# A SwiGLU feed-forward with seven half-block products in place of eight, and its down projection moved behind all gates

## The reference

```python
hn = rmsnorm(x, ln_mix_pre)
x = x + rmsnorm(stick_breaking_mixer(hn, w_qkv, w_o), ln_mix_post)
hn = rmsnorm(x, ln_ffn_pre)
g, u = jnp.split(hn @ w_gu, 2, axis=-1)      # 1024 x 1024 @ 1024 x 5632
y = (jax.nn.silu(g) * u) @ w_down            # 1024 x 2816 @ 2816 x 1024
x = x + rmsnorm(y, ln_ffn_post)
```

## Time and profile before

| | us |
|---|---|
| median of 3 runs | 1355.73 |
| lowest, highest | 1354.17, 1356.25 |
| span of the profiled execution | 1353.8 |
| PE busy | 1317.0 (97%) |
| DVE, ACT, POOL busy | 709.7, 541.8, 330.8 |

### The profile page before, as it was taken

The page is one execution under the profiler, slowest core; times in us unless marked ns, Lnnn a source line. Parts: engine busy times, 40 slices in busy tenths (PEclk is TensorE's granted clock), DMA queues, the critical chain, the costliest instruction groups (busy, mean ns, idle before and its releaser), DMA issues.

```text
span 1353.8 us, 18027 instructions
## 1 busy us (share of the span) xinstructions
PE 1317.0 (97%) x6648; PEld 1112.7 (82%) x6648; DVE 709.7 (52%) x880; ACT 541.8 (40%) x964; POOL 330.8 (24%) x229
## 2 busy tenths in 40 slices
PE   6999999999999988999999999999999999999998
PEld 6888888888888876778888888888888888888886
DVE  7699989898998997435104131313122222223227
ACT  5667767677777774324221211121202121111122
POOL 2111011101101000552441423232323232323332
PEclk9999999999999998999999999999999999999999
DMA  5001000000000004320110202011111111111112
GB/s 217 17 31 32 17 32 32 15 31 31 16 31 31 16 1 140 104 68 31 32 66 28 78 16 77 24 69 43 50 46 62 43 50 46 46 47 47 47 47 109
DMA packets 18340, 66.72 MB, mean 49 GB/s; under 512 B 2032, under 2 KB 2032, under 8 KB 18288
## 3 DMA queue, kind: packets, MB, share of 16 engines
q1 hardware_dynamic: 16704, 60.30, 13.0%
q10 hardware_dynamic: 1584, 5.77, 1.2%
HBM read 61.87 MB, written 4.19 MB: 49 GB/s over the span
## 4 chain that ended last, share of the span: by engine, by line
PE 90%; DVE 5%; ACT 2%; POOL 2%; DMA 1%; issue 1%; ACTq 0%; SPq 0%; DVEq 0%; POOLq 0%
PE bank L1299 12%; PE bank L1303 12%; PE bank L1301 12%; PE bank L1141 6%; PE bank L1142 6%; PE bank L1143 6%; PE bank L1367 5%; PE bank L1368 5%; PE bank L1366 5%; PE bank L1241 4%; PE bank L1215 3%; PE bank L1217 2%; PE bank L1261 2%; PE bank L1260 2%; PE bank L1189 1%; PE bank L1190 1%
## 5 line engine op out<-in xcount | busy, mean ns | idle before, releaser
L753 POOL TENSOR_TENSOR w_lo<-raw,w_hi 128x1024 fp32r<-128x1024 f32 x86 | 209.4, 2439 | 822.4 <-ACT w_hi L469 822.1
L1299 PE MATMUL bank<-hnT_hi,w_hi 128*128 128x512 f32 (+1 forms) x712 | 276.0, 388 | 0.0
L1301 PE MATMUL bank<-hnT_lo,w_hi 128*128 128x512 f32 (+1 forms) x712 | 275.6, 387 | 0.0
L1303 PE MATMUL bank<-hnT_hi,w_lo 128*128 128x512 f32 (+1 forms) x712 | 275.6, 387 | 0.0
L1046 DVE TENSOR_TENSOR sg<-bank,sg 128x512 f32<-128x512 f32 x44 | 30.4, 692 | 428.1 <-ACT sg L684 428.1
L469 ACT ACTIVATE w_hi<-raw 128x1024 fp32r<-128x1024 f32 x88 | 92.2, 1059 | 394.7 <-PE bank L1303 344.2
L949 DVE TENSOR_TENSOR_SCAN stay<-stay,diag_one 128x256 f32<-128x256 f32 (+7 forms) x128 | 180.4, 1409 | 3.7 <-ACT stay L585 3.7
L1301 PEld LDWEIGHTS bank<-hnT_lo,w_hi 128*128 128x128 f32 x712 | 134.1, 188 | 27.1
L1303 PEld LDWEIGHTS bank<-hnT_hi,w_lo 128*128 128x128 f32 x712 | 134.0, 188 | 27.2
L1299 PEld LDWEIGHTS bank<-hnT_hi,w_hi 128*128 128x128 f32 x712 | 134.1, 188 | 27.0
L1060 DVE TENSOR_TENSOR y<-bank,y 128x512 f32<-128x512 f32 x160 | 108.4, 690 | 82.5 <-PE bank L1368 75.4
(11 more groups left out here) (125 smaller groups left out, 2109.3 us busy)
## 6 DMA issues: line engine op xcount, KB each, us to landing
raw<-in_units SPq DMA_DIRECT2D x98, 512.0 KB, 3.2
acc<-in_x SPq DMA_DIRECT2D x8, 512.0 KB, 9.4
x_in<-in_x ACTq DMA_DIRECT2D x8, 512.0 KB, 3.3
out<-y SPq DMA_DIRECT2D x7, 512.0 KB, 2.6
g_pre_s<-in_mix_pre SPq DMA_DIRECT2D x1, 512.0 KB, 5.3
g_post_t<-in_mix_post ACTq DMA_DIRECT2D x1, 512.0 KB, 4.4
g_ffn_t<-in_ffn_pre ACTq DMA_DIRECT2D x1, 512.0 KB, 3.5
g_out<-in_ffn_post ACTq DMA_DIRECT2D x1, 512.0 KB, 3.5
```

Source lines behind the costliest of these rows:

```text
L753: nc.gpsimd.tensor_tensor(w_lo[slot], raw[:, raw_slot, :], w_hi[slot].bitcast(F32), ALU.subtract).then_inc(w_ready, 1)
L1299: nc.tensor.matmul(dst, wh, hnT_hi[:, kt, cols], start=(kt == 0 and b == 0), stop=False, skip_group_check=halves > 1)
L1301: nc.tensor.matmul(dst, wh, hnT_lo[:, kt, cols], start=False, stop=False, skip_group_check=halves > 1)
L1303: mm = nc.tensor.matmul(dst, wl, hnT_hi[:, kt, cols], start=False, stop=last, skip_group_check=halves > 1)
```

## The change

**Algorithm.** For a group the product hn (1024 x 1024) by 256 columns of gate (or up) is seen as a 2x2 by 2x2 block product: A11, A12, A21, A22 are token half by feature half, B11, B12, B21, B22 feature half by column unit. Winograd's form needs seven half-block products (12 matmuls each) in place of eight: P1 = A11·B11, P2 = A12·B21, P3 = S4·B22, P4 = A22·T4, P5 = S1·T1, P6 = S2·T2, P7 = S3·T3, with sums S of the A blocks and T of the B blocks. There are 22 such sets (gate and up of 11 groups); set 0 still uses eight products. The down projection is done in the same form at the end, for all groups at once: seven products of 11 steps each (12 matmuls a step).

**What it takes.** DVE forms S1..S4 of the activations (`pair_sums`), PE transposes seven operands in place of four (28 units of four transposes in place of 16), DVE forms T1..T4 of each set (`weight_sum`), the hidden sums S1..S4 (`hidden_sums`) and the combinations of the products (`joined`); POOL forms the T sums of the down weights (`weight_sums`). SBUF no longer holds everything: `x2` is stored to DRAM (`x2d`) as soon as it is made and read back late; the hidden operands (`hops`, 7 x 256 KB per group) and down weight sums (`wsums`, 4 x 256 KB per group) are stored to DRAM and loaded again step by step, as two 256 KB loads per step. The normed tile is written over `x2` in place, so `hn(t)` waits for the store of `x2` of that tile, except for the last tile, which has a buffer of its own. The loops over groups are unrolled.

```diff
+PRODUCTS = [("P1", 0, "A11"), ("P6", 1, "S2"), ("P5", 2, "S1"), ("P7", 3, "S3"),
+            ("P2", 4, "A12"), ("P3", 5, "S4"), ("P4", 6, "A22")]
...
+DOWN = [("P1", 0), ("P6", 1), ("P2", 0), ("P5", 1), ("P7", 0), ("P3", 1), ("P4", 0)]
...
+            for t in range(NT):
+                sp.wait_ge(x2_ready, t + 1)
+                sp.dma_start(x2d[t].rearrange("p (k c) -> p k c", c=P), x2(t)).then_inc(x2_out[t], 16)
...
+            for s in range(NSETS - 2):
+                if s and s % 2 == 0:
+                    store_hidden(s // 2 - 1)
+                raw_read(s)
+                load_set(s + 2)
+                if s % 2:
+                    store_wsums(s // 2)
+                    load_down(s // 2 + 1)
...
+            for n in range(RAWS, STEPS):
+                if n == NG - 1:
+                    store_hidden(NG - 1)
+                sp.wait_ge(hl_ready, n - RAWS + 1)
+                load_step_h(n)
+                sp.wait_ge(wl_ready, n - RAWS + 1)
+                load_step_w(n)
...
+            def step_hi(n):
+                k = n % NG
+                if n < NG:
+                    act.wait_ge(prod_full, prod_count(NSETS - 1, SLOT_AFTER[k]))
+                else:
+                    act.wait_ge(step_full, n - NG + 1)
+                act.wait_ge(hraw_in[n % RAWS], 16 * (n // RAWS + 1))
+                nc.scalar.activation(slot[k][0][:, :], hraw[:, n % RAWS, :], ACT.Copy).then_inc(hh_ready, 1)
+                act.wait_ge(wraw_in[n % RAWS], 16 * (n // RAWS + 1))
+                nc.scalar.activation(slot[k][2][:, :], wraw[:, n % RAWS, :], ACT.Copy).then_inc(wh_ready, 1)
...
             def hn(t):
                 dve.wait_ge(rstd_done, NT + 2 * t + 2)
+                if t < NT - 1:
+                    dve.wait_ge(x2_out[t], 16)
...
             for t in range(NT - 1):
                 if t + 3 < NT:
                     o_lo_sub(t + 3)
                 mix_scale(t)
+                if t >= 3:
+                    norm_low((2 * t - 6, 2 * t - 5))
...
-                if t < RING:
+                if t < 6:
                     hn(t)
+                if t in (4, 5):
+                    pair_sums(t - 4)
+            hn(6)
+            pair_low(0, 0, 3)
+            mix_scale(NT - 1)
+            pair_low(0, 3, 5)
+            pair_sums(2)
+            pair_low(1)
+            weight_sum(0, "T3", 1)
+            weight_sum(0, "T2", 0)
+            pair_low(2)
+            hn(7)
+            pair_sums(3)
+            weight_sum(0, "T1", 2)
+            weight_sum(0, "T4", 3)
+            pair_low(3)
...
+            def product(dst, k, left, start):
+                left_hi, left_lo = op[left]
+                for kt in range(4):
+                    w_h, w_l = (w[:, kt * P:(kt + 1) * P] for w in (wh(k), wl(k)))
+                    nc.tensor.matmul(dst[:, :], w_h, left_hi[:, kt, :], start=(start and kt == 0), stop=False,
+                                     skip_group_check=True)
+                    nc.tensor.matmul(dst[:, :], w_h, left_lo[:, kt, :], start=False, stop=False,
+                                     skip_group_check=True)
+                    mm = nc.tensor.matmul(dst[:, :], w_l, left_hi[:, kt, :], start=False, stop=(kt == 3),
+                                          skip_group_check=True)
+                mm.then_inc(prod_full, 1)
...
             for t in range(2, NT - 1):
                 out_project(t)
+                if t >= 3:
+                    norm_transpose(2 * t - 6)
+                    norm_transpose(2 * t - 5)
...
+            for s in range(1, NSETS):
...
+                product(b1, 0, "A11", True)
...
+                product(b6, 1, "S2", True)
...
+                product(b5, 2, "S1", True)
...
+                product(b7, 3, "S3", True)
+                pe.wait_ge(f_lo, w_count(s, 4))
+                pe.wait_ge(p1_done, s + 1)
+                product(b1, 4, "A12", False)
+                pe.wait_ge(f_lo, w_count(s, 5))
+                pe.wait_ge(comb, comb_count(s, "v"))
+                product(b5, 5, "S4", False)
+                pe.wait_ge(f_lo, w_count(s, 6))
+                pe.wait_ge(comb, comb_count(s, "c22"))
+                product(b7, 6, "A22", False)
```

More of the change, by code:

```diff
@@ L448, in _ @@
                 sp.dma_start(raw[:, n % 2, :], units[unit_row(n)]).then_inc(raw_in[n % 2], 16)
[L449 to L453, removed]
+            for e in range(2):
+                sp.wait_ge(w_ready, UNITS1 + e - 1)
+                sp.dma_start(raw[:, e, :], units[gate_unit(e)]).then_inc(raw_in[e], 16)
@@ L690, in _ @@
[L690 to L718, removed]
@@ L720, in _ @@
[L720 to L735 removed]
+            pair_hi(1)
@@ new lines, in _ @@
+            act.wait_ge(prod_full, prod_count(0, "P1"))
+            sum_hi(0, "T2", 0)
+            sum_hi(0, "T3", 1)
+            pair_hi(2)
+            sum_hi(0, "T1", 2)
+            sum_hi(0, "T4", 3)
+            pair_hi(3)
+            act.wait_ge(t_full, T_END)
+            act.wait_ge(x2_out[NT - 1], 16)
+            act.wait_ge(prod_full, prod_count(0, "P2"))
+            sigmoid(0, bank[0][:, :])
+            act.wait_ge(prod_full, prod_count(0, "Q2"))
+            sigmoid(1, bank[1][:, :])
@@ new lines, in _ @@
+            act.wait_ge(prod_full, slot_free(0, 0))
+            for e in range(2):
+                act.wait_ge(f_in[2 + e], 16)
+            block_hi(1, "B11", 0)
+            act.wait_ge(comb, comb_count(0, "c21"))
+            sigmoid(0, H21)
+            sum_hi(1, "T3", 3)
+            act.wait_ge(comb, comb_count(0, "c22"))
+            sigmoid(1, H22)
+            sum_hi(1, "T2", 1)
+            sum_hi(1, "T1", 2)
+            block_hi(1, "B21", 4)
+            block_hi(1, "B22", 5)
+            sum_hi(1, "T4", 6)
@@ L1016, in mix_scale, with norm_low, pair_low @@
                                                    op0=ALU.mult, op1=ALU.mult).then_inc(mix_scaled, 1)
-            def norm_tile(t):
-                for half in range(2):
-                    norm_lo(T_TRANS + 2 * t + half, t, half)
+            def norm_low(units_):
+                for u in units_:
+                    n = norm_unit(u)
+                    t_lo_sub(n, norm_dest(u, 1), norm_bank(n)[:, :].rearrange("p (k c) -> p k c", k=4),
+                             norm_dest(u, 0))
+            def pair_low(p, a=0, e=5):
+                norm_low(range(NT + 5 * p + a, NT + 5 * p + e))
@@ new lines, in down_sum @@
+            def down_sum(out_ap, bank_ap, sb):
+                nc.vector.tensor_tensor(out_ap, bank_ap, sb, ALU.add).then_inc(y_sum, 1)
+            LEFT, RIGHT = slice(0, HALF), slice(HALF, D)
+            for n in range(6, STEPS):
+                step_lo(n)
+                done, last = divmod(n + 1, NG)
+                if last == 0 and done >= 3 and done != 4:
+                    dve.wait_ge(step_full, n - NG + 1)
+                    for t in range(4):
+                        if done == 3:
+                            dve.wait_ge(y_copy, t + 1)
+                            down_sum(u2d[:, t, :], bank[4 + t][:, :], y(t)[:, LEFT])
+                        elif done == 5:
+                            dve.wait_ge(y_sum, t + 1)
+                            down_sum(y(4 + t)[:, RIGHT], bank[4 + t][:, :], u2d[:, t, :])
+                        elif done == 6:
+                            dve.wait_ge(y_sum, 4 + t + 1)
+                            down_sum(y(4 + t)[:, RIGHT], bank[t][:, :], y(4 + t)[:, RIGHT])
+                        else:
+                            down_sum(y(t)[:, RIGHT], bank[4 + t][:, :], u2d[:, t, :])
@@ L1418, in _ @@
-            for u in range(4):
-                for k in range(4):
-                    down_last(k, u)
-            for k in range(4, 2 * NT):
-                for u in range(4):
-                    down_last(k, u)
+            pair_transpose(0)
+            pe.wait_ge(mix_scaled, 2 * (NT - 1))
+            pe.wait_ge(t_lo, norm_unit(NT))
+            pe.wait_ge(f_lo, w_count(0, "B11"))
+            product(bank[0], 0, "A11", True)
+            pair_transpose(1)
+            pe.wait_ge(p1_done, 1)
```

921 lines of the change are left out of this document (613 added, 308 removed).

## The result

The changed kernel takes **1298.58 us** (median of four runs, 1297.64 to 1300.11) against 1355.28 for the kernel before (now four runs, 1354.17 to 1356.25): a ratio of 0.9581, 95% interval 0.9569 to 0.9593. The forecast was 1288.0, the range 1275 to 1310: the direction and most of the amount are right, 10.6 us of the forecast gain did not come. The time lies where rival A had it (1296 to 1312).

A forecast was written before the change was run, and what follows sets the result against it. PE was taken as the bound, its count alone giving 1271.9 us. Summed, 668 + 1.5 + 21 x 19.05 + 209.6 + 7.0 = 1286.2 as a span, 1.9 more for the median: 1288 us, range 1275 to 1310.

The forecast's parts named there:

- rival A: Transition: the x2 store is much dearer than taken, or more waits come; 8 to 24 us more, 1296 to 1312; chance 0.15.
- What PE loses: Feed-forward on PE: 384 matmuls gone at 0.2268 us, 87.1 us; 48 transposes added, 5.2 us.
- The transition: Attention to feed-forward: x2 stores landing at 4 us and sums lengthen each tile's chain; set 1 starts at 668.
- my own sign: Transition: the forecast is wrong if x2's stores land at 6 us or later.
- My bounds: x2 store: 2.6 us if its 512-byte pieces cost nothing, 12.1 us if each costs what a packet did.
- Set 1: Start of set 1: T2's split stands behind a combination, sigmoid, copy and two subtractions, about 4.2 against 2.7; 1.5 us lost.
- The steady sets: Gate and up sets: 19.05 us each, stalls put at nothing; DVE and POOL shared work 35.1 of 38.1 us per two sets.
- Down stage and tail: Down projection and end: 924 matmuls take 209.6 us at 2.72 a step, no load waits; tail 7.0, give or take 1.
- B: Sets: DVE and POOL's shared access, or ACT's order, stalls each by 1 to 2 us; 1308 to 1328; chance 0.08.
- C: Transition costs little more than before, as the store takes 2.6 to 2.9; 1278 to 1282 likely; chance 0.10.
- D: Down stage: loads don't run beside each other, 4.4 us a step against 2.72; 129 us more, 1417; chance 0.06.
- E: PE: waits fill the gaps, busy time stays near 1317; total within 1345 to 1356; chance 0.03.

The follow-up runs named there:

- the repaired kernel: Changed kernel with the x load behind the x2 store on SP, hn one tile later on DVE, and T2 first in set 1: 1280.62 us.
- experiments 8 and 6: 8: ring of two raw buffers not four, 1321.62 us; 6: product P1 done twice in sets 1 to 21 and down steps, 1382.09 us; both against the changed kernel.
- experiment 2: Changed kernel with the x load issued by SP ahead of the x2 store, in place of by ACT: 1297.96 us, ratio 0.9573.

## Why the prediction was right, and where it wasn't

- **What PE loses.** Right: 443 matmuls per 100 us as before, and putting the 384 back costs 83.5 us, 87.1 less the stall that they hide.
- **The transition.** The shape was right and one term of the sum was mis-sized. "I take 4.0" for the store of `x2`, "since the nearest row is a store of the same bytes in the same direction". It measured 5.86, 7.17, 6.00 and 3.17 for tiles 3 to 6, beside 5.92 for tile 2: 6.2 us more over the four. By my own sign (stores landing at 6 us or later) the step was wrong. `mix_scale(4)`, (5) and (6) started at 600.5, 615.7 and 629.7 where 598.2, 610.1 and 622.0 were forecast; PE's P1 of set 0 was 6.8 us late and set 1 7.9. The row taken was of stores with nothing beside them. My bounds thought of the pieces only; that the load of x is issued at the same moment stands in the code, and was costed at nothing, without a word on what covers it. Its pieces cost little: 3.2 alone against 2.6 for a store in whole rows. The Trainium skill's rule on small descriptors (DMA: Bandwidth & Descriptors, "Why small descriptors are slow"), from which I had estimated 2.9, was closer to a store alone than my 4.0.
- **Set 1.** The place and the releaser (T2's split on POOL) were right, the size was 1.5 against 4.2: 2.67 of wait and some 1.6 of slow matmuls behind it, which I had put to the transition alone. The wait was mis-sized because the sum had the sigmoid and a copy in it, which are not in the chain, and left out the two T sums on DVE (1.3 us); and the two splits took 3.3 us and not 2.6.
- **The steady sets.** Right as a price (nothing), with cover of 5.3 us forecast and found: POOL's split ended 16.5 into the set against 16.4 to 17. "It fits, but barely" is shown too, though 35.1 of 38.1 was reckoned with durations; with distances from start to start it is 33.3. That cover is less than it looks, since work put into it delays its own start: two operations, 2.5 us, used all of the 5.3.
- **Down stage and tail.** Right: 209.2 us for the 924 matmuls, no wait, the 4 MB load landing in 17.6; the last matmul starts at 1289.32 and the span ends 7.0 us later.
- **Rivals.** A came true at its low edge and for a cause it did not name. B did not come: the changed kernel has no stall from set 2 on, but with four POOL operations more a set it has 3.7 us of them. C is refuted as the kernel stood, but the repaired kernel reaches 1280.6, within it. D and E are refuted (experiments 8 and 6).

The span of 1296.3 stands 2.3 us under the median; 1.9 was taken. The errors do not cancel: nearly all of them lie on the late side.

## What to carry to other kernels

When a wait for a transfer is added, look not for what such a transfer took somewhere, but for what is issued at that moment on any queue; moving the neighbour behind it was worth 10 us here, as much as leaving the transfer out. Before more work is put on DVE and POOL, add up both engines' SBUF operations by their distances from start to start: up to the period it is nearly free, past it every microsecond and more is paid. A short wait on PE can cost more than its length, but not always: behind the same 2.67 us wait in set 1, five of the six kernels that have it lost another 1.6 to 1.8 us in seven matmuls 0.42 us apart, and that of experiment 2 lost 0.2.

## What the runs showed that was not expected

- Two 512 KB transfers on two queues, issued 0.01 us apart, made the store 5.9 to 7.2 us; with none beside it it was 3.2, and 5.3 to 5.6 with both on one queue, the load first. The total is nearly that of one after the other.
- 256 KB loads land in 3.6 us with four of a kind under way and in 2.7 with two; two still carried 211 GB/s, over the 193 that a step of 2.72 us needs.
- With the store gone, POOL's two splits ahead of a 1/rms and then PE's own output projections set the time: removing the store is worth no more than shortening it to 3.3 us.
- The wait of set 1 had a different end in the kernel of experiment 2. The granted clock is 1.00 in the 10 us behind it there (680 to 690), and 0.83 in the changed kernel (681 to 691), where the matmuls 0.42 us apart are at the lower level (1.2 GHz). The runs do not show why.
```profile
679.90 0.50 PE L1805 MATMUL bank<-S_hi,wh 128*128 128x512 f32 x1 [2.67 <-POOL wl L1115]
680.24 0.39 PE L1807 MATMUL bank<-S_lo,wh 128*128 128x512 f32 x1
```
